# Four projections of the first state-space group move into the recurrence's last two turns

## The reference, cut to what matters

```python
rw_x, z_x, xbc_x, dt_x, gate_x = jnp.split(hx @ w_in[l], IN_SPLITS, axis=-1)
rw_c, z_c, xbc_c, dt_c, gate_c = jnp.split(hc @ w_in[l], IN_SPLITS, axis=-1)
ya_x, _, _ = rwkv7_branch(centred_token_shift(rw_x, rw_mu[l]), s_fwd, s_bwd, *rw_params)
...
xbc = jax.nn.silu(centred_depthwise_conv(xbc, conv_w) + conv_b)      # x (2048), B (8x128), C (8x128)
dt = jax.nn.softplus(dt_raw + dt_bias);  log_a = -jnp.exp(a_log) * dt
y_f, h_f = ssd_chunked(xs * dt[..0..], log_a[..0..], bm, cm, h0_fwd)  # and backwards, flipped
mix_x = merge_branches(ya_x, gated_group_rmsnorm(yb_x, z_x, ssm_norm_w[l]), gate_x, ...)
x = x + g1x * rms_norm(mix_x, norm_post1[l])
x = x + g2x * rms_norm(peer_ffn(h2x, ...), norm_post2[l])
```

## Time and profile before

| | |
|---|---|
| median of 3 runs | 3932.25 us (3930.14 to 3936.12) |
| profiled execution | 3928.69 us, span 3926.9 us |
| TensorE busy | 3530.5 us, 90% |
| VectorE busy | 1864.1 us, 47% |
| ScalarE busy | 683.9 us, 17% |
| GpSimd busy | 1133.0 us, 29% |
| recurrence, turns 15 and 16 | 1307.2 to 1416.2 us |
| state-space stage | 1416.2 us to 2022.0 us |

### The profile page before, as it was taken

The page is one execution under the profiler, slowest core; times in us unless marked ns, Lnnn a source line. Parts: engine busy times, 40 slices in busy tenths (PEclk is TensorE's granted clock), DMA queues, the critical chain, the costliest instruction groups (busy, mean ns, idle before and its releaser), DMA issues. The chain is left out here.

```text
span 3926.9 us, 72072 instructions
## 1 busy us (share of the span) xinstructions
PE 3530.5 (90%) x30735; PEld 2121.6 (54%) x30735; DVE 1864.1 (47%) x3194; ACT 683.9 (17%) x1242; POOL 1133.0 (29%) x1734
## 2 busy tenths in 40 slices
PE   7999999999999789999999999989877777777776
PEld 3456666666666546666688888475332323333332
DVE  1334544544544448877830000156465565564644
ACT  2223223223223112122210000011110110100101
POOL 2044344334335201001000000024444444444442
PEclk9999999999999889999999999999999999999998
DMA  9322222222222157776753435359999999999997
GB/s 381 111 70 76 62 71 73 64 71 71 66 71 66 48 166 247 223 254 200 231 191 141 171 129 207 125 236 427 395 427 428 428 427 428 428 427 428 428 427 311
DMA packets 473389, 906.04 MB, mean 231 GB/s; under 512 B 85180, under 2 KB 307086, under 8 KB 403854
## 3 DMA queue, kind: packets, MB, share of 16 engines
q0 software_dynamic: 73728, 536.90, 32.5%
q1 hardware_dynamic: 307664, 318.46, 24.6%
q10 hardware_dynamic: 91710, 46.43, 4.0%
HBM read 889.04 MB, written 12.68 MB: 230 GB/s over the span
## 5 line engine op out<-in xcount | busy, mean ns | idle before, releaser
L2558 PE MATMUL ps<-w_slots,diag 128*128 128x512 f32 x1920 | 899.4, 615 | 257.9 <-DMA w_slots<-in_peer_v,ixv 224.6
L2558 PEld LDWEIGHTS ps<-w_slots,diag 128*128 128x128 f32 x1920 | 356.8, 194 | 798.5 <-issue 465.8
L994 PE MATMUL ps<-hT,w_slots 128*128 128x512 f32 (+1 forms) x1536 | 617.8, 536 | 4.2 <-PEq L230 2.2
L1684 PE MATMUL ps<-hT,w_slots 128*128 128x256 f32 (+1 forms) x1504 | 497.5, 487 | 6.9 <-PEq L655 4.9
L2171 POOL DMA_INDIRECT w_slots<-in_peer_v,ixv x244 | 264.6, 1084 | 596.8 <-PE ps L2558 513.5
L2335 DVE SCALAR_TENSOR_TENSOR junk<-w_slots,hT 128x2048 f32<-128x2048 f32 x128 | 293.5, 2293 | 271.2 <-DMA w_slots<-in_peer_u,ixu 267.2
L2335 DVE SCALAR_TENSOR_TENSOR junk<-ybT,hT 128x2048 f32<-128x2048 f32 x128 | 293.4, 2292 | 263.5 <-DMA ybT<-in_peer_u,ixu 263.0
L1684 PEld LDWEIGHTS ps<-hT,w_slots 128*128 128x128 f32 x1504 | 284.1, 191 | 180.2 <-issue 159.3
L994 PEld LDWEIGHTS ps<-hT,w_slots 128*128 128x128 f32 x1536 | 270.7, 189 | 169.7 <-issue 144.9
L724 POOL TENSOR_TENSOR Ypart<-Ym,Sm 128x126 f32<-128x126 f32 (+22 forms) x496 | 190.3, 384 | 491.5 <-DMA Sm<-s_blocks 453.9
L2428 ACT ACTIVATE diag<-ident,coef 128x128 f32<-128x128 f32 x240 | 94.6, 401 | 904.6 <-PE ps L2558 892.4
(11 more groups left out here) (382 smaller groups left out, 4378.2 us busy)
## 6 DMA issues: line engine op xcount, KB each, us to landing
w_slots<-in_w_mod SPq DMA_DIRECT2D x128, 512.0 KB, 5.7
w_slots<-in_w_in SPq DMA_DIRECT2D x56, 1024.0 KB, 6.1
w_slots<-in_w_in ACTq DMA_DIRECT2D x44, 1024.0 KB, 7.7
w_mod_ring<-in_w_mod SPq DMA_DIRECT2D x16, 2048.0 KB, 13.6
w_slots<-in_w_in SPq DMA_DIRECT2D x7, 4096.0 KB, 13.9
w_slots<-in_w_branch_a SPq DMA_DIRECT2D x4, 4096.0 KB, 14.0
w_slots<-in_w_branch_b SPq DMA_DIRECT2D x4, 4096.0 KB, 13.8
w_slots<-in_w_out SPq DMA_DIRECT2D x4, 4096.0 KB, 12.7
```

Of the source, the lines that this page charges most:

```text
L994: last = mm(ps[:, 4, t0:TOK], w[m % 2][:, k, :], hT[:, k, t0:TOK], start=(k == 0), stop=(k == KC - 1))
L1684: last = mm(out, w[m % SLOTS_W][:, k, :], hT[:, k, t0:TOK], start=(k == 0), stop=(k == KC - 1))
L2558: last = nc.tensor.matmul(ps[:, 4 * n + c, :], diag[:, k % 2, :], vb[k % NB][:, c * 512:(c + 1) * 512], start=False, stop=False)
```

## The change

- Turn 15 projects x0 in the k pieces (as before), x1 in the r pieces and dt in the v pieces. Turn 16 projects C in the k pieces, and z0 and z, which are put after the outputs; z0's first 5 steps stand before var, its other 11 and the 16 of z behind it. Before, these pieces of r and v were empty, and the k pieces of turn 16 held dt.
- SP loads the weights of z0, C, z (turn 15) and B (turn 16) in the recurrence; the state-space stage no longer loads B and C at its start, nor z0 and z from ACT.
- In state-space group 0 TensorE projects only B, in its old place in the order. The turning of dt and the sums over it stand among B's steps and behind them; before they stood among x1's steps and behind them.
- The first tile of group 1 goes into bank 1, where C of group 0 now waits, and needs the mark p3 as before. The gate of group 0 lies in banks 2 and 3, so TensorE waits for the mark z of group 0 before tx0 and tx1.
- var goes to bank 6 instead of 7 and no longer waits for ACT's n1; the product for the bonus no longer waits for std.

```diff
+                    if i == PAIRS - 1:
+                        sp.wait_ge(*ss_early.by("x0", 0))
+                        sp.dma_start(w[0], w_in[:, :, Z0:Z0 + P]).then_inc(ss_loads[0], 16)
+                        sp.wait_ge(*PB.by("wu3", i))
+                        sp.dma_start(w[3], w_in[:, :, C0:C0 + P]).then_inc(ss_loads[3], 16)
+                        sp.wait_ge(*ss_early.by("x1", 0))
+                        sp.dma_start(w[1], w_in[:, :, Z0 + P:Z0 + 2 * P]).then_inc(ss_loads[1], 16)
+                    if i == PAIRS:
+                        sp.wait_ge(*VB.by("zt1", PAIRS - 1))
+                        sp.dma_start(w[2], w_in[:, :, B0:B0 + P]).then_inc(ss_loads[2], 16)
...
+                EARLY = {"x0": (0, 1, ps[:, 4, :]), "x1": (1, 1, ps[:, 5, :]), "C": (3, 1, ps[:, 1, SEQ:TOK]),
+                         "z0": (0, 2, ps[:, 2, SEQ:TOK]), "z": (1, 2, ps[:, 3, SEQ:TOK])}
...
-                        elif name == "k":
-                            (next_tile if B else step_sizes)(k0, k1)
+                        elif B and name == "v":
+                            step_sizes(k0, k1)
+                        elif B:
+                            early_tile({"k": "x0", "r": "x1"}[name], k0, k1)
+                        else:
+                            early_tile({"k": "C", "r": "z0", "v": "z"}[name], k0, k1)
...
+                    if Z and not B:
+                        outputs(1, z, i)
+                    if A or B:
+                        piece("r", 0, 4)
...
-                    piece("v", 4, 6)
+                    if B or A:
+                        piece("v", 4, 6)
+                    else:
+                        piece("r", 0, 5)
                     if Z:
-                        need(pe, AA, "n1", p)
                         need(pe, AD, "std", z - 1)
                         pe.wait_ge(*AD.by("ysq", z))
-                        mm(ps[:, 7, 0:SEQ], head_mean[:, :], ysq[:, :], start=True, stop=True).then_inc(*PD.did("var"))
+                        mm(ps[:, 6, SEQ:TOK], head_mean[:, :], ysq[:, :], start=True, stop=True).then_inc(*PD.did("var"))
+                    if not A and not B:
+                        piece("r", 5, KC)
+                        piece("v", 0, 6)
...
-                        act.wait_ge(*PA.by(TILES[n], i))
-                        tile(act, 6 * i + n + SLOTS_W)
+                        act.wait_ge(*projected(TILES[n]))
+                        if i or n > 1:
+                            tile(act, 6 * i + n + SLOTS_W)
...
-                        if A and (n, i) != (0, 0):
+                        if A and (i or n == 2):
                             project(n, i, k0, k1)
...
                     if B:
+                        if g == 0:
+                            pe.wait_ge(*AA.by("z", 0))
                         turned("tx0", 0, 2, g)
                         turned("tx1", 1, 3, g)
```

## The result

| | before | after |
|---|---|---|
| median, 18 runs each | 3931.64 us (3924.44 to 3941.81) | 3938.94 us (3934.25 to 3946.27) |
| profiled execution | 3928.69 us, span 3926.9 us | 3941.65 us, span 3939.9 us |
| TensorE busy | 3530.5 us | 3517.2 us |

The ratio is 1.0019, with a 95% interval of 1.0012 to 1.0027: some 7 us slower, 5 to 11 by the interval, clear of no change but small. The forecast was 3942.6 us.

A forecast was written before the change was run, and what follows sets the result against it. VectorE's 44.43 us after the sums were taken to bound group 0, TensorE the pace from there. Terms +7.9 - 2.3 - 0.5 + 5.3 = +10.4 us gave 3939.1 us profiled, 3942.6 us as median; range 3934 to 3948.

The forecast's parts named there:

- turn 15, to the chain's start: Turn 15: x1 and dt steps before `solved` overrun the old hole; its end moves from 1376.91 to 1383.6, +6.7 us.
- turn 16's chain: Turn 16: chain steps with C's half-width steps between them take 17.3 us against 25.5 us, -8.2 us.
- outputs and copy: Behind turn 16's chain: the outputs and ACT's copy take 5.39 us as before.
- mean to the next stage: Mean to the state-space stage's first matmul: with z0 and z there, 17.8 us against 8.4 us, +9.4 us.
- VectorE's start in the stage: Group 0: sums begin 14.7 us into the stage instead of 16.97 us, so VectorE begins 2.3 us sooner.
- VectorE's stretch: Group 0: VectorE's 44.43 us behind the sums stay, less 0.5 us of waiting for w_mod transfers.
- restart and new order before `rows`: Start of group 1: tx0, tx1 and 3 steps stand behind mark z, with a half-clock restart: +5.3 us.
- rival A: Neither turn 16's end nor group 1's start is cold: -4.0 us, 3938.6 us, no measurable change; chance 0.13.
- rival B: Group 0: the w_mod waits vanish and VectorE ends 6.1 us sooner than forecast: 3936.5 us, no change; chance 0.08.
- The full count of 35.1 us: Group 0: TensorE's removed 35.1 us count in full because VectorE is not the bound: 3905 us; chance 0.02.
- the stage no later: Moved work fits into the 11.59 us hole and the 4.92 us at the end: 3934.7 us, no change; chance 0.03.
- D: Turn 16 goes cold as a whole, C offering half of dt's columns: up to 10 us more, 3952.6 us; chance 0.09.

The follow-up runs named there:

- after_early_trip: The changed kernel with the running sums' transfer through DRAM started ahead of w_mod piece 6 instead of behind the 11th: 3936.76 us, ratio 1.0008.
- the thin kernels: The changed kernel and the kernel before, each with VectorE's group 0 mods cut from 512 columns to 64: 3930.54 us and 3924.14 us.
- lean_early_trip: Against the kernel before, only dt (turn 15) and C (turn 16) moved; sums during x1, running sums stored early: 3928.77 us, ratio 0.9988.
- before_sums_early_trip: The kernel before with the sums over dt at step 10 of x1 and the running sums sent through DRAM earlier: 3923.37 us, ratio 0.9985.
- before_sums_sooner: The kernel before with the sums over dt behind 10 of x1's 16 steps instead of all: 3930.22 us, ratio 0.9996.
- after_steps_first: The changed kernel with all of x0's steps of group 1 ahead of the two transposes: 3942.00 us, ratio 1.0027.
- after_gate_back: The changed kernel with z0 and z put back into group 0, behind the sums: 3933.48 us, ratio 0.9999.

## Why the prediction was right

The time is 3.7 us below the forecast and well within the range; the forecast's own mechanism, slower by some 10 us, is what the trace shows. By the prediction's own measure, that 7.9 us are what can be told from no change, the 7.3 us of the medians fall just short of the "slower" to which it gave 0.60; the interval of the ratio leaves no change out all the same. Its sum, term by term:

| term | predicted | trace of after |
|---|---|---|
| turn 15, to the chain's start | +6.7 | +9.2 (7.7 without the slow x1) |
| turn 16's chain | -8.2 | -8.0 |
| outputs and copy | 0 | -0.3 |
| mean to the next stage | +9.4 | +9.0 |
| VectorE's start in the stage | -2.3 | -2.6 |
| VectorE's stretch | -0.5 | -0.6 |
| restart and new order before `rows` | +5.3 | +4.5 |
| sum at `rows(0)` | +10.4 | +11.2 (9.7) |

At the mixing stage it is 10.7 us, or 9.2 without the slow x1. The medians show 7.3 us, with 4.7 to 10.6 by the interval. The 9.2 us lie within it and the 10.7 just outside; a better number than that I don't have. That the sum at `rows(0)` is off by 0.8 us only is in part luck: turn 15 came out 2.5 us dearer, and the other terms together 1.7 us cheaper.

**Turn 15** was sized too small by 1.0 us even without the slow x1. In the six variants with x1 there, the mean comes 21.3 to 22.1 us behind the outputs, as predicted. From the mean to the chain it is 23.5 to 24.3 us, 23.47 in the trace of after, and not a regular turn's 22.09. Which of the small products makes the difference was not tried.

**The clock** (rival A) was as unkind as assumed at group 1's start: 0.50 in the window of the transposes. It was so at turn 16's end as well, where z0's first ten records took 4.00 us, 0.40 each and not 0.22. At the start of the stage it was kind, as the sum had it: 3.75 us became 1.96. The cost behind mean came out at 17.39 us for 17.8. The section "Loop structure matters more than you think" of the Trainium skill's page "TensorE: Matmul & The Clock Gate" says that matmuls which wait between bursts run cold and that work kept back-to-back stays warm, and it is borne out on both sides here: work at 0.50 behind 31.55 and 8.28 us of idle time, and the stage's start at full clock behind 11.82 us without a gap.

**w_mod** (rival B) did not happen. 5.9 us of waiting stayed, 4.7 of them behind the trip of the running sums; after_early_trip showed that it is the trip. **The full count of 35.1 us** (C) and **the stage no later** (E) are ruled out by the trace; that TensorE's work counts in group 0 once VectorE is shorter was seen in the thin kernels, and there it was worth 6.5 us. **D**, the cold chain, did not happen in this kernel: turn 15's end, full of dt's steps, hands the chain over at full clock. It did in lean_early_trip.

**What the prediction did not see.** "TensorE and DVE end group 0 within a microsecond" was read as two engines with equally much work. before_sums_early_trip shows that TensorE's side held 5.3 us of waits and lower clock, which go when the sums come sooner and the trip is early. The forecast did not depend on it, since the change makes TensorE's time in group 0 shorter than VectorE's in either case, but a forecast for a kernel with a faster VectorE would have gone wrong.

## What to carry to other kernels

Work taken off an engine in a stretch that another engine sets gains nothing there, and costs what does not fit into holes where it goes: here the 35 us of matmuls made the stage start 9.9 us later (8.4 without the slow x1). The idle time that it left, 31.55 and 8.28 us, ended in a restart at half clock. Ask first which event starts the engine that sets the stretch, and move that: here the sums and one small transfer, a few lines each, gained 5.8 us, and the moving of 35 us of matmuls lost 7. Before calling two engines balanced, add up the waits and the clock in the busier one's time.

## What was not expected of the hardware

- Pauses of TensorE of 1 to 2.5 us did not all have the same effect. Right before `rows`, 1.01 us went with 1.95 us for its records and no longer way to the mixing stage. In before_sums_sooner 1.53 us went with 2.90 us, a granted clock of 0.76 in 1478 to 1484 and 2.9 us more to the mixing stage. In lean_early_trip, behind 2.50 us, the records of `rows` ran in 1.95 us, and only the six of x0 behind them took 4.14 us instead of 2.74. Behind the 1.99 us in the kernel before, the clock was 0.95 over 1440 to 1460, with TensorE busy all the time.
- Unbroken work did not always bring the full clock back soon: in after_steps_first TensorE was busy for all of 1486 to 1496, with transposes, one-column products and small ones first, and had 0.50 throughout. Small products with pauses between them can lose it: in lean_early_trip, with 8.27 of 15 us busy, it was 0.50 in 1375 to 1390. With more of dt's steps between the same products (after_gate_back, 12.86 of 15 us busy) it kept 1.00.
- Two loads of 1 MB that ACT issued one after the other held ACT for 2.63 us in the changed kernel, where a single one takes 0.39, and the gate's Silu behind them, for which TensorE waits there, started after 2.27 us of idle time that the timeline puts down to issue. The kernel before has the same, 2.58 us, where nobody waited for it.
